# A two-block transformer kernel: 80 of 96 modulation units move from branch A's matmuls to VectorE and ScalarE beside the feed-forwards

## The chip, the cores and the metric

The kernel runs on one core of one Trainium2 chip. The metric is the device time of one execution in microseconds (us). Before the change three runs took 2449.18, 2457.3 and 2463.91 us, median 2457.3.

## The reference, cut to what matters

256 tokens of width 1024 go through a first block of two layers and a second block of two layers, all in fp32. A layer of the first block has three mixing branches (A a recurrent scan, B a chunked linear attention, C a sparse attention), a merge, and a feed-forward with a width-3 convolution over time. The second block modulates each layer by a vector that depends only on a condition `c`:

```
cond = silu(c)                                        # (1024,)
for layer in range(2):
    mod = cond @ ada_w[layer] + ada_b[layer]          # 1024 x 6144 each
    sh1, sc1, g1, sh2, sc2, g2 = split(mod, 6)
    h = rms_norm(x) * (1 + sc1) + sh1
    x = x + g1 * hybrid_mixer(h, ...)                 # GLA heads and retention heads
    x = x + g2 * ffn(rms_norm(x) * (1 + sc2) + sh2)   # layer 0 dense, layer 1 eight experts

def conv_glu(h):                                      # first block
    up = pad(h @ w_up)                                # 2 before the first token
    c = conv_b + sum(conv_w[j] * up[:, j:j + seq] for j in range(3))
    gate, val = split(c)
    return (silu(gate) * val) @ w_down                # hidden width 2816
```

In the mixer, the 16 columns `ga` of the projection feed `log_sigmoid(ga @ w_alpha + b_alpha)`, the decay of the GLA heads.

## The kernel before, in words

Activations lie with the channels on the partitions, 8 tiles of 128 by 256 tokens. Weights come in units of 128x1024 fp32 (512 KB). SyncE loads them in one fixed order (`ORDER.loads`) into `ring`, which has six slots: load n waits until unit n-6 has been used. Most are split units (kind "s"). To keep fp32 accuracy, each is split in two on the way: ScalarE rounds it to `w_high` (`high_to`, L1746), VectorE subtracts to get `w_low` (`low_to`, L2276), each into one of six slots again, and TensorE runs 24 matmuls of 256 columns for it: high by high, high by low, low by high for 8 pieces. ScalarE may round unit n only after TensorE has multiplied unit n-6, VectorE may take it after ScalarE, TensorE after VectorE.

Each engine's program is written out by hand and runs in that order, so what stands behind a wait waits too. The places that matter here:

- Branch A (`branch_a` in the programs of TensorE, VectorE and ScalarE) is a chain of small products of 64x64 whose results are taken out of PSUM by ScalarE or VectorE before the next may begin. Between its steps `mod_point` puts work that doesn't depend on it: the modulation matmuls. A raw unit (kind "r", not split) holds 128x1024 of `ada_w`; TensorE multiplies it with a column of `cond` broadcast to 32 columns (tiles `ring`, `cond` in the trace). 48 units a layer, in three rounds of 16, four at a point; after each round ScalarE copies the bank to `rope`, TensorE transposes it, ScalarE takes it to `mod`.
- The feed-forwards (`feed_forward`) run over 22 groups of 128 hidden channels, three units a group: two up (gate and value) and one down. TensorE runs up(j), then down(j-2). ScalarE, per group: rounds three units, waits for up(j), writes gate and value with bias (L2066, L2067), waits for VectorE's taps, Sigmoid (L2069), waits for the product, rounds it to `hid_high` (L2075). VectorE, per group: three `w_low`, then the taps (four operations of 254 or 255 columns, L2317) once ScalarE has written gate and value, two multiplications (L2308), `hid_low`. The feed-forward of the second block has no taps.
- In the second block's mixer (`linear_attention`) TensorE computes `ga` with 16 plain fp32 matmuls whose weights have 16 columns (`w_ga`, from the tile of constants), VectorE copies it out, and two matmuls give alpha.

Of the kernel before, what the change touches and what calls it, by code (L numbers as in the profile page):

```python
# [33 lines left out]
def _columns(table, sizes):  # L34
# [13 lines left out]
    ("ret_g", 4), ("ret_b", 4), ("w_ga", 128), ("w_alpha", 256)])  # L48
# [64 lines left out]

class Order:
# [5 lines left out]
    RAW1 = MOD_UNITS + 1  # L120
    QK2, RQK2, RV2, GV2, GR2, RG2, OUT2, FEED2 = 0, 4, 12, 16, 20, 24, 28, 36

    def __init__(self):
        self.loads = []
        for layer in range(LAYERS):
            self._load("s", self.layer1(layer), self.A_V)
            self._load("r", layer * self.RAW1, 1)
            self._load("s", self.layer1(layer) + self.A_V, self.C - self.A_V)
            self._load("r", layer * self.RAW1 + 1, MOD_UNITS)
            self._load("s", self.layer1(layer) + self.C, self.LAYER1 - self.C)  # L130
        for layer in range(LAYERS):
            self._load("s", self.layer2(layer), self.FEED2 + (EXPERTS * EXPERT_UNITS if layer else 3 * FF_GROUPS))
# [38 lines left out]
    @staticmethod  # L171
    def fed_ahead(j, groups):

        return 5 if j == 0 else min(3 * j + 4, 3 * groups - 1)

# [72 lines left out]
class Rounds:  # L248

    ROUND = 2 * KT

    def __init__(self):
        self.taken, self.stage = 0, 0

    def more(self, n):
        r, at = self.stage // 3, self.stage % 3
        if at == 1:
            self.stage += 1  # L260
            return r, True, range(0)
        if at:
            return r, False, range(0)
        first, self.taken = self.taken, min(self.taken + n, (r + 1) * self.ROUND, MOD_UNITS)
        return r, False, range(first, self.taken)

    def out(self):
        r, at = self.stage // 3, self.stage % 3
        if (at == 0 and self.taken == (r + 1) * self.ROUND) or at == 2:
            self.stage += 1  # L270
            return r, at
        return r, None

    def open(self):
        return self.stage < 3 * MOD_UNITS // self.ROUND


# [6 lines left out]
        "turned0 turned1 turned2",  # L284
    "mod_act":
        "full0 out0 full1 out1 full2 out2",
# [88 lines left out]
        "ga alpha swapped0 sc00 sc01 sc10 sc11 swapped1 turned s0 s1 s2 intra0 intra1 kturned0 y kturned1 rs0 "  # L375
# [84 lines left out]
def build(nc, a_x, a_pos, a_cond, a_const, a_par1, a_par2, a_router, a_norms, a_weights, a_moe, a_out):  # L460
# [167 lines left out]
    for w in tmps:  # L628
# [49 lines left out]


# [60 lines left out]
    of_mod, of_a, of_b, of_c, of_merge, of_ffn, of_add = (  # L740
        [stage(name, layer) for layer in range(LAYERS)]
        for name in ("mod", "a", "b", "c", "merge", "ffn", "add"))
# [54 lines left out]
    def tensor_program():  # L797
# [99 lines left out]
        def mod_point(M, A, rounds, layer, n=4):  # L897
            r, turn, units = rounds.more(n)
            if turn:
                pe.wait_ge(*M.act(f"full{r}"))  # L900
                for i in range(4):
                    ins = pe.transpose(psum[7][:, i * P:(i + 1) * P], rope[:, i * P:(i + 1) * P], c_("ident"))
                ins.then_inc(*M.pe.mark(f"turned{r}"))
            for j in units:
                k, block = j % Rounds.ROUND // 2, j % 2
                if j % Rounds.ROUND == 0:
                    pe.wait_ge(*(M.act(f"out{r - 1}") if r else A.dve("kk_scaled")))
                raw = layer * ORDER.RAW1 + 1 + j
# [8 lines left out]
        def branch_a(R, A, M, side, layer):  # L917
            s0, rounds, VT = ORDER.layer1(layer), Rounds(), PA[:, 8:12, :]
# [42 lines left out]
            low = layer * ORDER.RAW1  # L961
# [434 lines left out]
        def linear_attention(L, side, layer):  # L1396

            wga = par2(layer, "w_ga").rearrange("p (k r) -> p k r", r=16)
# [81 lines left out]
            fill(side, 3)  # L1480
# [215 lines left out]
        for layer in range(LAYERS):  # L1696
            R, M, A, B, C, G = (d[layer] for d in (of_mix, of_mod, of_a, of_b, of_c, of_merge))
# [19 lines left out]
        for layer in range(LAYERS):  # L1717
            L, s0 = of_lin[layer], ORDER.layer2(layer)
            if layer:
# [3 lines left out]
            begin(of_mix2[layer].dve, [(one.s, half(one.bank, 0), True), (one.s + 1, half(one.bank, 1), False),  # L1723
                                       (two.s, half(two.bank, 0), True)])
# [11 lines left out]
    def scalar_program():  # L1736
# [75 lines left out]
        def branch_a(A, M, side, layer):  # L1812
            s0, a, rounds = ORDER.layer1(layer), A.act, Rounds()
            WA, GD = PA[:, 12, :], PA[:, 13, :]

            def point():
                rounds.more(4)
                r, step = rounds.out()
                if step == 0:
                    act.wait_ge(s_raw, layer * ORDER.RAW1 + (r + 1) * Rounds.ROUND + 1)  # L1820
                    act.activation(rope, psum[7][:, :], Copy).then_inc(*M.act.mark(f"full{r}"))
                elif step == 2:
                    act.wait_ge(*M.pe(f"turned{r}"))
                    src = psum[7][:, :].rearrange("p (i q s) -> p q i s", i=4, q=4)[:, :, :, 0:1]
                    dst = mod[:, 16 * r:16 * r + 16].rearrange("p (q i o) -> p q i o", q=4, o=1)
                    act.activation(dst, src, Copy).then_inc(*M.act.mark(f"out{r}"))
# [32 lines left out]
            act.wait_ge(s_raw, layer * ORDER.RAW1 + 1)  # L1859
# [195 lines left out]
        def feed_forward(F, s0, groups, conv=None, ahead=False, rotary=None):  # L2055
            for j in range(groups):
# [18 lines left out]
                act.activation(HH[:, ts_], HD[n], Copy).then_inc(*f.mark("high"))  # L2075
                if rotary is not None and j == 3:
                    act.wait_ge(*rotary.dve("angle"))
                    act.activation(rope[:, T:2 * T], angle, Sin).then_inc(*rotary.act.mark("sin"))
                    act.activation(reduced, angle, Sin, scale=0.5).then_inc(*rotary.act.mark("half_sin"))
            if ahead:  # L2080
# [136 lines left out]
        for layer in range(LAYERS):  # L2217
            s0 = ORDER.layer1(layer)
            R, M, A, B, C, G = (d[layer] for d in (of_mix, of_mod, of_a, of_b, of_c, of_merge))
# [20 lines left out]
            feed_forward(of_conv[layer], s0 + ORDER.FEED, FF_GROUPS, layer, ahead=True,  # L2240
# [3 lines left out]
        for layer in range(LAYERS):  # L2244
# [10 lines left out]
            if layer == 0:  # L2255
                feed_forward(of_feed, s0 + ORDER.FEED2, FF_GROUPS, ahead=True)
# [10 lines left out]
    def vector_program():  # L2267
# [138 lines left out]
        def branch_a(A, M, side, layer):  # L2406
# [147 lines left out]
            dve.wait_ge(*M.act("out2"))  # L2554
            copy(d, raw_mod[:, layer * MOD_UNITS:(layer + 1) * MOD_UNITS], mod)
# [288 lines left out]
        def feed_forward(F, S, s0, groups, conv=None, scale=None, ahead=False, rotary=None):  # L2844
            for j in range(groups):
# [3 lines left out]
                low_to(s0 + ORDER.fed_ahead(j, groups))  # L2849
                if conv is not None:  # L2850
                    tap = lambda i: par1(conv, "taps", j * TAPS + i)
                    dve.wait_ge(*F[j].act("taken"))
                    for back in (1, 2):
                        for h, (out, src) in enumerate(((CG[n], gate), (CV[n], value))):
                            if back == 2:
                                dve.wait_ge(f.sem, f.last()[1] - 1)
                            stt(f, out[:, back:T], src[:, 0:T - back], tap(4 * h + 2 - back), out[:, back:T], MUL, ADD,
                                "read" if back == 2 and h else "-")
                    dve.wait_ge(*F[j].act("sig"))
# [3 lines left out]
                else:  # L2863
# [3 lines left out]
                    tt(f, HD[n], SG[n], value, MUL, "product")  # L2867
                dve.wait_ge(*F[j].act("high"))
# [13 lines left out]
        def linear_attention(L, side, layer, last):  # L2882
# [35 lines left out]
            dve.wait_ge(*L.pe("ga"))  # L2918
# [255 lines left out]
        def modulation(S, layer):  # L3174
            d = S.dve
            tt(d, mod, raw_mod[:, layer * MOD_UNITS:(layer + 1) * MOD_UNITS], par2(layer, "ada_b"), ADD)
# [9 lines left out]
        for layer in range(LAYERS):  # L3186
            s0 = ORDER.layer1(layer)
            R, M, A, B, C, G = (d[layer] for d in (of_mix, of_mod, of_a, of_b, of_c, of_merge))
# [18 lines left out]
            feed_forward(of_conv[layer], of_add[layer], s0 + ORDER.FEED, FF_GROUPS, layer, ahead=True,  # L3207
# [4 lines left out]
        for layer in range(LAYERS):  # L3212
# [11 lines left out]
            if layer == 0:  # L3224
                feed_forward(of_feed, of_add2, s0 + ORDER.FEED2, FF_GROUPS, scale=lambda dt: mod[:, 40 + dt:41 + dt],
# [160 lines left out]
```

## Time and profile before

| | |
|---|---|
| median of 3 runs | 2457.3 us |
| the profiled execution | 2458.52 us, its span 2457.1 us, about 1.4 us around it |
| TensorE (PE) busy | 2270.8 us, 92% |
| VectorE (DVE) busy | 1602.9 us, 65% |
| ScalarE (ACT) busy | 1174.1 us, 48% |
| HBM read | 423.08 MB, 173 GB/s over the span |
| granted TensorE clock | 0.958 of full on the mean |

TensorE's matmuls are pipelined: one of 256 columns is shown with 0.28 us, but the next starts 0.12 us after it. So durations of matmuls are read from start to start. The feed-forwards of the first block lie at about 472 to 663 us and 1128 to 1320 us, that of the second at 1495 to 1690 us; branch A lies at about 20 to 175 us and 680 to 829 us, and the points with modulation matmuls in it from 64.6 us and from 719.8 us on.

### The profile page before, as it was taken

What the parts mean: (1) busy time and instruction counts of PE and PEld (TensorE: products, weight loads), DVE (VectorE), ACT (ScalarE), POOL (GpSimd) and SP (SyncE); (2) the same over time, 40 slices, a digit from 0 to 9 for tenths busy, and PEclk for the clock granted to TensorE, in tenths of its full rate; (3) what the DMA queues carried; (4) which work ended last, traced back from release to release, by engine and by line L of the source; (5) the groups of instructions that cost most, each with busy time, mean ns of one, the idle gap of its engine ahead of it and who ended that gap; (6) DMA issues with size and microseconds to landing.
All of it is one profiled execution on the core that took longest, in us unless ns stands there. A gap on an engine that the chain in (4) does not pass through costs nothing.

```text
span 2457.1 us, 44886 instructions
## 1 busy us (share of the span) xinstructions
PE 2270.8 (92%) x19011; PEld 2046.4 (83%) x19011; DVE 1602.9 (65%) x2442; ACT 1174.1 (48%) x1703; POOL 0.2 (0%) x4
## 2 busy tenths in 40 slices
PE   7789788999998888889999989999989999999998
PEld 7469788999976787889998989998988888877776
DVE  6537776688773587666776756555765554477886
ACT  5234534455552354344655435444444443456665
POOL 0000000000000000000000000000000000000000
PEclk9999898999999998989998989999988999999999
DMA  5664333355446542334654425563413554579995
GB/s 206 250 237 157 114 103 112 129 198 194 150 172 240 209 145 86 120 111 139 196 199 137 143 64 179 181 185 135 145 35 111 191 182 181 176 271 324 322 327 194
DMA packets 118634, 427.06 MB, mean 174 GB/s; under 512 B 13344, under 2 KB 16160, under 8 KB 118304
## 3 DMA queue, kind: packets, MB, share of 16 engines
q1 hardware_dynamic: 116016, 421.81, 50.0%
q8 instruction: 150, 2.46, 0.4%
q10 hardware_dynamic: 2416, 2.37, 0.3%
q14 instruction: 52, 0.43, 0.1%
HBM read 423.08 MB, written 1.05 MB: 173 GB/s over the span
## 4 chain that ended last, share of the span: by engine, by line
PE 76%; DVE 15%; ACT 5%; issue 3%; DMA 2%; SPq 0%; ACTq 0%; DVEq 0%
PE bank L801 75%; DVE w_low L2276 4%; DVE arena L2308 4%; DMA ring<-in_weights 2%; DVE arena L2317 1%; ACT w_high L1746 1%; DVE y_mix L2308 1%; DVE arena L2813 1%; PE bank L1631 1%; ACT arena L2025 1%; DVE arena L2312 0%; DVE arena L2314 0%; DVE small L2811 0%; DVE arena L2327 0%; ACT arena L1970 0%
## 5 line engine op out<-in xcount | busy, mean ns | idle before, releaser
L2276 DVE TENSOR_TENSOR w_low<-ring,w_high 128x1024 fp32r<-128x1024 f32 x700 | 822.8, 1219 | 156.6 <-ACT w_high L1746 155.8
L1746 ACT ACTIVATE w_high<-ring 128x1024 fp32r<-128x1024 f32 x700 | 699.8, 1051 | 168.8 <-PE bank L801 159.4
L801 PE MATMUL bank<-u_high,w_high 128*128 128x256 f32 x2576 | 740.2, 287 | 29.7 <-DVE u_low L2308 19.7
L801 PE MATMUL bank<-u_low,w_high 128*128 128x256 f32 x2576 | 731.8, 284 | 0.0
L801 PE MATMUL bank<-u_high,w_low 128*128 128x256 f32 x2576 | 731.4, 284 | 0.0
L801 PEld LDWEIGHTS bank<-u_high,w_high 128*128 128x128 f32 x2576 | 496.6, 193 | 43.8 <-issue 35.5
L801 PEld LDWEIGHTS bank<-u_low,w_high 128*128 128x128 f32 x2576 | 496.4, 193 | 0.1
L801 PEld LDWEIGHTS bank<-u_high,w_low 128*128 128x128 f32 x2576 | 495.4, 192 | 0.0
L801 PE MATMUL bank<-arena 64*64 64x64 f32 (+5 forms) x4456 | 240.5, 251 | 77.6 <-issue 20.8
L801 PEld LDWEIGHTS bank<-arena 64*64 64x64 f32 (+2 forms) x4456 | 210.0, 155 | 115.9 <-issue 62.0
L2308 DVE TENSOR_TENSOR arena<-arena 128x256 f32<-128x256 f32 (+3 forms) x218 | 141.7, 666 | 46.7 <-ACT arena L2069 21.3
L801 PE MATMUL bank<-w_high,u_high 128*128 128x256 f32 (+1 forms) x480 | 165.2, 344 | 0.0
L801 PE MATMUL bank<-w_low,u_high 128*128 128x256 f32 (+1 forms) x480 | 162.4, 338 | 0.0
L801 PE MATMUL bank<-w_high,u_low 128*128 128x256 f32 (+1 forms) x480 | 162.1, 338 | 0.0
L801 PE MATMUL bank<-hid_high,w_high 128*128 128x256 f32 x528 | 148.1, 280 | 0.9 <-DVE w_low L2276 0.9
L801 PE MATMUL bank<-hid_high,w_low 128*128 128x256 f32 x528 | 147.9, 280 | 0.0
L801 PE MATMUL bank<-hid_low,w_high 128*128 128x256 f32 x528 | 147.9, 280 | 0.0
L2308 DVE TENSOR_TENSOR turned_low<-bank,turned_high 128x256 fp32r<-128x256 f32 (+1 forms) x66 | 24.8, 399 | 158.5 <-ACT turned_high L2181 158.4
L2181 ACT ACTIVATE turned_high<-bank 128x256 fp32r<-128x256 f32 (+1 forms) x66 | 22.2, 365 | 219.9 <-PE bank L1631 219.9
L1752 ACT ACTIVATE arena<-bank 128x512 f32<-128x512 f32 (+1 forms) x72 | 42.1, 584 | 146.3 <-PE bank L801 146.2
L2317 DVE SCALAR_TENSOR_TENSOR arena<-bank,params,arena 128x255 f32<-128x255 f32 (+1 forms) x204 | 85.4, 474 | 38.5 <-ACT arena L2067 23.3
L801 PE MATMUL bank<-w_high,turned_high 128*128 128x512 f32 x242 | 99.7, 412 | 8.2 <-DVE w_low L2276 7.0
(307 smaller groups left out, 3057.9 us busy)
## 6 DMA issues: line engine op xcount, KB each, us to landing
ring<-in_weights SPq DMA_DIRECT2D x534, 512.0 KB, 4.5
ring<-in_moe SPq DMA_DIRECT2D x264, 512.0 KB, 5.2
const<-in_const SPq DMA_DIRECT2D x1, 2619.0 KB, 16.5
out<-x_res ACTq DMA_DIRECT2D x2, 512.0 KB, 3.0
x_res<-in_x SPq DMA_DIRECT2D x1, 512.0 KB, 5.2
x_res<-in_x ACTq DMA_DIRECT2D x1, 512.0 KB, 5.7
const<-in_par ACTq DMA_DIRECT2D x1, 462.0 KB, 3.4
params<-in_par ACTq DMA_DIRECT2D x1, 247.0 KB, 10.4
```

The costliest lines, as they stand in the source:

```text
L801: return pe.matmul(out, lhsT, rhs, start=start, stop=stop, skip_group_check=loose)
L1631: ins = pe.transpose(bank(q, tile)[:, f * P:(f + 1) * P], hid_e[q % 2][tile][:, f * P:(f + 1) * P], c_("ident"))
L1746: act.activation(WH[:, ORDER.slot[cut], :], weights("s", cut), Copy).then_inc(s_hi, 1)
L1752: act.activation(job.dst, held(job), Copy).then_inc(s_out["act"], 1)
L2025: act.activation(L_c[a][:, h, :], L_c[a][:, h, :], Exp, bias=neg_max[a][:, h:h + 1], accum_out=exp_sum[a][:, h:h + 1]).then_inc(*c.mark(f" ...
L2181: act.activation(HTH[q % 2][tile][:, 0:n], psum[4 + 2 * (q % 2) + tile][:, 0:n], Copy)\
L2276: dve.tensor_tensor(WL[:, b, :], weights("s", cut), WH[:, b, :].bitcast(f32), SUB).then_inc(s_lo, 1)
L2308: dve.tensor_tensor(out, a, b, op).then_inc(*t.mark(name))
L2317: dve.scalar_tensor_tensor(out, a, s, b, op0, op1).then_inc(*t.mark(name))
L2813: dve.match_replace(work_[:, a, 0:n], top8, work_[:, a, 0:n], -3e30).then_inc(*d.mark())
```

## The change

Only round 0 of layer 0 (16 of 96 modulation units) stays in branch A; the other rounds, with their copies to `rope` and transposes, are gone, and so are their loads there. The other 80 come as units of kind "m" in another layout: each holds 128 result channels by 1024, so that VectorE multiplies it with `cond` in a row of 1024 on all partitions (`cond_row`, itself loaded as one more unit per feed-forward) and ScalarE sums over the row (a copy with `accum_out`) into one column of `raw_mod`. They stand in the groups 3 to 21 of the three feed-forwards: 20, 20 and 40 of them. In the first block's feed-forwards `low_to` (three `w_low` a group) moves from before the taps to behind them. The 16 gate columns of GLA become a split unit of their own, padded to 128 columns and begun with the first units of the mixer.

```diff
+    ROUNDS1 = range(0, 1), range(1, 1)
+    ROWS = range(16, 36), range(36, 56), range(56, 2 * MOD_UNITS)
...
+    def _feed(self, g, first):
+        for j in range(FF_GROUPS):
+            before, last = self.fed_ahead(j - 1, FF_GROUPS) if j else -1, self.fed_ahead(j, FF_GROUPS)
+            self._load("s", first + before + 1, last - before)
+            of = self.modulated(g, j)
+            self._load("m", self.row1(g) + of[0] if len(of) else 0, len(of))
+    def modulated(self, g, j):
+        n = len(self.ROWS[g])
+        if j < 3:
+            return range(j == 1)
+        return range(1 + n * (j - 3) // (FF_GROUPS - 3), 1 + n * (j - 2) // (FF_GROUPS - 3))
...  TensorE, linear_attention
-            for k in range(KT):
-                for part in (UH, UL):
-                    ins = mm(psum[0][0:16, 0:T], wga[:, k, :], part[:, k, :].bitcast(f32),
-                             k == 0 and part is UH, k == KT - 1 and part is UL)
-            ins.then_inc(*L.pe.mark("ga"))
-            fill(side, 1)
             pe.wait_ge(*L.dve("ga"))
...
-            fill(side, 3)
+            fill(side, 4)
...  ScalarE, feed_forward
+            def row(j):
+                K, at = of_rows[g], ORDER.row1(g)
+                if j == 1:
+                    act.wait_ge(*arrived("m", at))
+                    act.activation(cond_row, weights("m", at), Sigmoid).then_inc(*K.act.mark("cond"))
+                for i in ORDER.modulated(g, j) if j > 2 else ():
+                    act.wait_ge(*K.dve(f"product{i}"))
+                    col = ORDER.ROWS[g][i - 1]
+                    act.activation(products[i % 3], products[i % 3], Copy, accum_out=raw_mod[:, col:col + 1])\
+                        .then_inc(*K.act.mark(f"sum{i}"))
...
                 act.activation(HH[:, ts_], HD[n], Copy).then_inc(*f.mark("high"))
+                row(1 if j == 1 else j - 1 if j > 3 else 0)
...  VectorE, feed_forward
-                low_to(s0 + ORDER.fed_ahead(j, groups))
+                if conv is None:
+                    low_to(s0 + ORDER.fed_ahead(j, groups))
                 if conv is not None:
...
+                    low_to(s0 + ORDER.fed_ahead(j, groups))
                     dve.wait_ge(*F[j].act("sig"))
...
                     tt(f, HD[n], SG[n], value, MUL, "product")
+                row(j)
                 dve.wait_ge(*F[j].act("high"))
```

ScalarE in the first block's feed-forward, one group from one `hid_high` to the next, before:

```order
L2075 ACTIVATE hid_high<-arena 128x256
L1746 ACTIVATE w_high<-ring 128x1024 x3
L2066 ACTIVATE arena<-bank,params 128x256
L2067 ACTIVATE arena<-bank,params 128x256
L2069 ACTIVATE arena<-arena 128x256
L2075 ACTIVATE hid_high<-arena 128x256
```

and now (L2126 is `hid_high`, L2104 the sum over the row of the group before, L1786 `w_high`, L2117 and L2118 gate and value, L2120 the Sigmoid):

```order
L2126 ACTIVATE hid_high<-arena 128x256
L2104 ACTIVATE arena,raw_mod<-arena 128x1024
L1786 ACTIVATE w_high<-ring 128x1024 x3
L2117 ACTIVATE arena<-bank,params 128x256
L2118 ACTIVATE arena<-bank,params 128x256
L2120 ACTIVATE arena<-arena 128x256
L2126 ACTIVATE hid_high<-arena 128x256
```

Nothing moved there but the sum, which came in ahead of the three roundings. VectorE in the same group, before (the first row is `w_low`, the second and third the taps, the fourth the two multiplications):

```order
L2276 TENSOR_TENSOR w_low<-ring,w_high 128x1024 x3
L2317 SCALAR_TENSOR_TENSOR arena<-bank,params,arena 128x255 x2
L2317 SCALAR_TENSOR_TENSOR arena<-bank,params,arena 128x254 x2
L2308 TENSOR_TENSOR arena<-arena 128x256 x2
L2308 TENSOR_TENSOR hid_low<-arena,hid_high 128x256
```

and now:

```order
L2371 SCALAR_TENSOR_TENSOR arena<-bank,params,arena 128x255 x2
L2371 SCALAR_TENSOR_TENSOR arena<-bank,params,arena 128x254 x2
L2330 TENSOR_TENSOR w_low<-ring,w_high 128x1024 x3
L2362 TENSOR_TENSOR arena<-arena 128x256 x2
L2362 TENSOR_TENSOR arena<-ring,arena 128x1024
L2362 TENSOR_TENSOR hid_low<-arena,hid_high 128x256
```

The three `w_low` now stand between the taps and the multiplications, and the product of the modulation unit between these and `hid_low`. TensorE in branch A of layer 1, where points follow each other most closely (`ring,cond` is a point's eight matmuls, `arena` and `const` the chain's), before:

```order
L801 MATMUL bank<-arena 64x64 x48
L801 MATMUL bank<-ring,cond 32x512 x8
L801 MATMUL bank<-arena 64x64 x16
L801 MATMUL bank<-ring,cond 32x512 x8
L801 MATMUL bank<-const,arena 64x64 x16
```

and now:

```order
L846 MATMUL bank<-arena 64x64 x96
L846 MATMUL bank<-const,arena 64x64 x16
```

The products of the chain now stand directly behind each other: 96 are the 32 ahead of the first of three points, the 48 and the 16.

## Rows read from the trace of the kernel before

**Rows 1.** The chain that ended last, shares of the span by engine.

```profile
PE 76%; DVE 15%; ACT 5%; issue 3%; DMA 2%; SPq 0%; ACTq 0%; DVEq 0%
```

**Rows 2.** Stretches: length, busy PE, PEld, DVE, ACT, POOL; clock, DMA share, GB/s.

```profile
486.00:586.00 100.00, 98.82 (x839) 98.41 (x838) 79.75 (x128) 59.48 (x90) 0.00 (x0) 1.00 0.55 185
586.00:662.00 76.00, 76.00 (x650) 76.00 (x649) 55.18 (x92) 41.02 (x62) 0.00 (x0) 1.00 0.52 174
1500.00:1690.00 190.00, 190.00 (x1604) 190.00 (x1603) 110.40 (x143) 89.90 (x123) 0.00 (x0) 1.00 0.55 172
```

**Rows 3.** ACT in order of time, first feed-forward: start, length, [idle before <-releaser].

```profile
485.33 0.56 ACT L2066 ACTIVATE arena<-bank,params 128x256 f32<-128x256 f32 x1 [6.34 <-PE bank L801]
...
499.34 0.55 ACT L2066 ACTIVATE arena<-bank,params 128x256 f32<-128x256 f32 x1
...
504.04 0.42 ACT L2075 ACTIVATE hid_high<-arena 128x256 fp32r<-128x256 f32 x1 [0.95 <-DVE arena L2308]
504.36 2.94 ACT L1746 ACTIVATE w_high<-ring 128x1024 fp32r<-128x1024 f32 x3
507.20 0.55 ACT L2066 ACTIVATE arena<-bank,params 128x256 f32<-128x256 f32 x1
507.65 0.55 ACT L2067 ACTIVATE arena<-bank,params 128x256 f32<-128x256 f32 x1
...
645.59 0.56 ACT L2066 ACTIVATE arena<-bank,params 128x256 f32<-128x256 f32 x1 [1.07 <-PE bank L801]
...
654.04 0.56 ACT L2066 ACTIVATE arena<-bank,params 128x256 f32<-128x256 f32 x1 [2.98 <-PE bank L801]
```

**Rows 4.** DVE in order of time, one group of the first feed-forward.

```profile
497.57 3.50 DVE L2276 TENSOR_TENSOR w_low<-ring,w_high 128x1024 fp32r<-128x1024 f32 x3 [0.53 <-ACT w_high L1746]
500.99 1.64 DVE L2317 SCALAR_TENSOR_TENSOR arena<-bank,params,arena 128x255 f32<-128x255 f32 x4
503.12 0.89 DVE L2308 TENSOR_TENSOR arena<-arena 128x256 f32<-128x256 f32 x2 [0.48 <-ACT arena L2069]
```

**Rows 5.** Groups by line and shape: busy, mean ns of one, idle before.

```profile
L2308 DVE TENSOR_TENSOR arena<-arena 128x1024 f32<-128x1024 f32 x41 | 49.5, 1220 | 5.7 <-ACT arena L2040 4.7 <-ACT arena L1792 0.4
L1970 ACT ACTIVATE arena<-arena 128x1024 f32<-128x1024 f32 x10 | 10.6, 1056 | 47.0 <-DVE arena L2308 47.0
L2025 ACT ACTIVATION_READ_ACCUMULATOR arena<-arena,small 128x1 f32 x32 | 6.0, 187 | 0.0
L801 PE MATMUL bank<-ring,cond 128*32 128x512 f32 x384 | 64.3, 638 | 14.4 <-DMA ring<-in_weights 7.2 <-DVE arena L2308 5.2 <-ACT mod L1826 1.5
```

**Rows 6.** PE in order of time, branch A of layer 1.

```profile
728.45 1.05 PE L801 MATMUL bank<-ring,cond 128*32 128x512 f32 x4 [0.61 <-DMA ring<-in_weights]
...
732.65 2.51 PE L801 MATMUL bank<-arena 64*64 64x64 f32 x78 [0.53 <-DVE arena L2308]
...
760.71 1.92 PE L801 MATMUL bank<-ring,cond 128*32 128x512 f32 x16
762.56 3.02 PE L801 MATMUL bank<-arena 64*64 64x64 f32 x96
...
769.44 1.05 PE L801 MATMUL bank<-ring,cond 128*32 128x512 f32 x4
...
774.61 1.15 PE L801 MATMUL bank<-const,arena 64*64 64x64 f32 x32
...
811.60 1.54 PE L801 MATMUL bank<-arena 64*64 64x64 f32 x43 [4.54 <-issue]
```

**Rows 7.** What PE waited for: us in total, times, longest us.

```profile
PE bank L801 <- issue: 21.2, 12, 4.5
```

**Rows 8.** Stretches, as in rows 2: clock in branch A, and the gate columns.

```profile
810.00:820.00 10.00, 8.40 (x170) 5.06 (x170) 1.96 (x6) 0.78 (x2) 0.00 (x0) 0.66 0.44 152
...
1345.40:1352.10 6.70, 6.70 (x32) 2.92 (x30) 1.07 (x2) 0.90 (x1) 0.00 (x0) 1.00 0.64 237
```

**Rows 9.** GB/s in the 40 slices of the span.

```profile
GB/s 206 250 237 157 114 103 112 129 198 194 150 172 240 209 145 86 120 111 139 196 199 137 143 64 179 181 185 135 145 35 111 191 182 181 176 271 324 322 327 194
```

More of the change, by code:

```diff
@@ L111, in constants, with __init__, more, out @@
     return c
+class Rounds:
+    ROUND = 2 * KT
+    def __init__(self, rounds):
+        self.first, self.last = rounds.start, rounds.stop
+        self.taken, self.stage = self.ROUND * self.first, 3 * self.first
+    def more(self, n):
+        r, at = self.stage // 3, self.stage % 3
+        if at == 1:
+            self.stage += 1
+            return r, True, range(0)
+        if at:
+            return r, False, range(0)
+        first, self.taken = self.taken, min(self.taken + n, (r + 1) * self.ROUND, self.last * self.ROUND)
+        return r, False, range(first, self.taken)
+    def out(self):
+        r, at = self.stage // 3, self.stage % 3
+        if (at == 0 and self.taken == (r + 1) * self.ROUND) or at == 2:
+            self.stage += 1
+            return r, at
+        return r, None
+    def open(self):
+        return self.stage < 3 * self.last
 class Order:
@@ L245, in made @@
         return jobs
[L248 to L275, printed above, removed]
 STEPS = {
@@ L677, in build @@
     CG, CV, SG, HD = ([new(T) for _ in TWO] for _ in range(4))
+    cond_row, products = at(32 * T, 4 * T), [at((36 + 4 * n) * T, 4 * T) for n in range(3)]
     space(0)
@@ L2079, in feed_forward @@
                     act.activation(reduced, angle, Sin, scale=0.5).then_inc(*rotary.act.mark("half_sin"))
+            row(groups - 1)
             if ahead:
@@ L2842, in branch_c, with feed_forward, row @@
             branches_b_c(B, C, G, level, probabilities, side, layer, last)
-        def feed_forward(F, S, s0, groups, conv=None, scale=None, ahead=False, rotary=None):
+        def feed_forward(F, S, s0, groups, g, conv=None, scale=None, ahead=False, rotary=None):
+            def row(j):
+                K, at = of_rows[g], ORDER.row1(g)
+                if j == 2:
+                    dve.wait_ge(*K.act("cond"))
+                    tt(K.dve, cond_row, cond_row, weights("m", at), MUL, "cond")
+                    prior(K.dve)
+                for i in ORDER.modulated(g, j) if j > 2 else ():
+                    dve.wait_ge(*arrived("m", at + i))
+                    if i > 3:
+                        dve.wait_ge(*K.act(f"sum{i - 3}"))
+                    tt(K.dve, products[i % 3], weights("m", at + i), cond_row, MUL, f"product{i}")
             for j in range(groups):
@@ L3175, in modulation @@
             d = S.dve
+            for n in (0, 1) if layer == 0 else (2,):
+                dve.wait_ge(*of_rows[n].act.end())
+            if layer == 0:
+                dve.wait_ge(*of_mod.act("out"))
             tt(d, mod, raw_mod[:, layer * MOD_UNITS:(layer + 1) * MOD_UNITS], par2(layer, "ada_b"), ADD)
```

114 lines of the change are left out of this document (67 added, 47 removed), and 13 rows, old and new, of the table STEPS.

## The prediction

> **What bounds the kernel now.** Read the chain of waits first. 76% of the span is TensorE and 15% VectorE [rows 1], so the time is TensorE's stream of work plus the places where it stands. Then the stretches. In the first block's feed-forward TensorE is busy all the time at full clock, VectorE 80% in the first part and 73% later, ScalarE 59 and 54% [rows 2]. By these shares there is room for more work beside the matmuls. The order of events inside one group shows how little. Up to some 580 us the gate writes of two groups start 7.86 us apart (499.34 and 507.20) and nothing there waits for TensorE; at the end they are 8.45 us apart (645.59 and 654.04) and each waits over 1 us for TensorE [rows 3]. So TensorE needs 8.45 us for three units (2.81 each), and ScalarE and VectorE, handing work to each other, need 7.86 us for a group. They wait for each other most of the rest of their time; the room is 0.6 us a group, not the 25% that the busy share leaves.
>
> **The loop in the first block's feed-forwards.** Before, VectorE's three w_low (3.42 us from start to start of what follows, 497.57 to 500.99) run while ScalarE still rounds the second and third unit and writes gate and value [rows 3, 4]. Afterwards they cannot: the taps stand ahead of them, the taps wait for gate and value, these stand behind three roundings, and the roundings behind hid_high of the group before. Walk round one full group, from the start of the gate write:
> - gate and value written: 1.05 (507.20 to the end of the second, 507.65 + 0.55) [rows 3]
> - taps, until the next may start: 1.57 (1.64 less the 0.07 by which neighbours overlap) [rows 4]
> - three w_low, now in the chain: 3.42 [rows 4]; the Sigmoid lies beside them, so its 0.48 is gone
> - two multiplications and the hand-over: 0.92 [rows 4]
> - hid_high: 0.33 (504.04 to 504.36) [rows 3]
> - the sum over the modulation row: a ScalarE operation of 128x1024 takes 1.056, its successor starts 0.1 earlier, and reading the accumulator (0.187 by itself) costs about 0.1 so overlapped [rows 5]: 1.05. The bound from below is 0.95, from above 1.25.
> - three roundings: 2.84 (504.36 to 507.20) [rows 3]
>
> The sum is 11.2 us where TensorE needs 8.45. The product of the modulation unit on VectorE (1.22 [rows 5]) lies where VectorE would wait for ScalarE (5.3 us from product to taps, against 1.2 + 0.4 of work), so it costs nothing. Without modulation rows the loop would be 10.1: moving w_low alone already makes it longer than TensorE's 8.45.
>
> A feed-forward has 22 groups. From the first gate write to the last, 21 steps, it takes 168.7 us now (485.33 to 654.04) [rows 3], and three units of TensorE behind that. Afterwards: the first two steps are short of one w_low each and of the sum (8.0 and 10.0); step 3 is 13.7, because the load six places behind the cond unit waits for VectorE to use that unit in group 2, and lands late for group 3's last rounding; step 4 is 10.1; then 16 of 11.2; the last 9.3. That is 230, and about 10 from the last gate write to TensorE's end instead of 8.4: +63. In the second layer 2 us of it were lost already to work on the rotary tables in the same loop, so +63 and +62, **+125**. Behind each, ScalarE's last sum and three roundings come before the squares of the norm: about 1 us each, **+2**. A row's cost of 0.95 or 1.25 would move the pair by -4 or +8.
>
> **The second block's feed-forward** has no taps; w_low stays at the front. The loop there: hid_high 0.33, two sums 2.1, one rounding 0.97, three w_low 3.42, multiplications 0.92, hand-over: 7.8, under 8.45 [rows 3 to 5]. TensorE stays the bound, nothing is added. 5.1 loads of 0.524 MB per 8.45 us are 317 GB/s, and the trace shows 322 to 327 held over slices [rows 9], so it fits barely: **+1**, bounds 0 and +9 (if only 300 GB/s come).
>
> **Branch A.** The modulation matmuls hold TensorE 64.3 us, and it stood 14.4 us before them [rows 5]: 78.7 for 96 units, 65.6 for the 80 that go. Not all comes back, since they also covered hand-overs. Taken point by point in layer 1: the first two points (719.8 to 732.65) return only 3.2, because VectorE's own chain to the masked products, started at the operation after "at", lets the next product begin at 729.4 instead of 732.65 [rows 6]. Where the chain's results are ready, a point returns all: 1.85 (760.71 to 762.56), 5.2 for the one that waited for loads (769.44 to 774.61) [rows 6]. All points of layer 1: 31.4, less 1.7 for two hand-overs that come bare (AKV0's copy 0.8, the last Pm's addition 0.85): 29.7. Layer 0, rounds 1 and 2: 25.2 less 2.0. Together 53. Against that two things: TensorE stands for instructions ("issue") 12 times, 21.2 us, all but little of it in stretches of small products [rows 7]; without the long matmuls more such waits come into the open, at a mean of 1.8 us I take three. And such a gap goes ahead of a fall of the clock: after 4.54 us without instructions the granted clock of 810 to 820 us is 0.66 [rows 6, 8], some 3 us lost in ten; once more. I take **-47**, between -35 and -55.
>
> **Gate columns.** 32 passes with 16-column weights take 6.7 us [rows 8]; the padded unit takes 2.81. But alpha now follows directly, while VectorE first takes out a bank (0.6) and then ga (0.4): TensorE stands 1.1 us where a side job of 5.6 us covered it. -2.8 a layer, **-5.6**.
>
> **Sum.** 125 + 2 + 1 - 47 - 5.6 = +75. On the profiled execution's 2458.5 us (span 2457.1), which lies 1.2 above the median, that is 2534; against the median 2533. I forecast 2534.
>
> **Rivals.**
> - TensorE stays the bound of the convolution's feed-forwards, faster. VectorE's work per group is 6.3 us and becomes 7.5, ScalarE's 4.7 becomes 5.7, both under 8.45 [rows 2, 4]. It needs ScalarE to be able to write gate and value before VectorE's product of the group before, which the written order forbids. Time: 2458.5 - 47 - 5.6 = 2406. By the Trainium skill, "Perfetto Trace Analysis", section "Identifying the Most-Contended Engine", the busy share of VectorE and ScalarE is a fair measure of how close they are to their limit; by that rule this rival would hold. The 7.86 us loop at 80% busy [rows 2, 3] speaks against reading it so here. 6%.
> - Slower loop, smaller: the sum over the row hides (ScalarE waits for something else at that point), the step is 10.1: 2 x 19 x 1.05 less, 2494. Nothing in rows 3 shows such a wait. 8%.
> - The clock falls in the feed-forwards. TensorE now stands 2.7 us in every group, and in branch A a gap of 4.5 went ahead of a fall [rows 6, 8]. As long as half clock lasts a third of the time, the 2.7 us that TensorE has to spare take it. If it is half throughout, three units take 16.9 us, and 2 x 20 x 5.7 are added: 2760; if half of the groups are hit so, 2648. 6%. The Trainium skill, "TensorE: Matmul & The Clock Gate", section "HAM oscillation — how this bites in real kernels", tells of a kernel in which waits between bursts cooled the clock every time; it speaks for this rival, and the rows only show single falls.
> - Branch A gives little: waits for instructions and for VectorE fill the room. -20 instead of -47: 2561. Rows 7 speak for it, the rows of layer 1 where results lay ready against. 10%.
> - Loads bind in both kinds of feed-forward (landing late behind the modulation units): +9 in the second block, about +15 in each of the others if a load takes 7 us: 2573. 8%.
>
> **Numbers.** My case has 62% and a range of its own of 2515 to 2552. The range 2494 to 2570 takes in the second rival and the fourth; out of it are the first, the third, the far half of the last. 0.5% is 12 us, about what a measurement of this kernel can tell. Slower by more than that 0.92, within it 0.02, faster 0.06.
>
> **What would show it.** In the first block's feed-forwards gate writes 11.2 us apart, with TensorE waiting 2.7 us per group for w_low, and VectorE waiting some 3.5 us for gate and value ahead of the taps. In the second block's 8.45 and no such wait. Branch A of layer 1 some 30 us shorter from kk_spread to y, of layer 0 some 23, less the waits for instructions. I am wrong if the steps are 8.45, if ScalarE's sum takes much over 1.1, or if branch A keeps its length.

## The result, and the profile after

The changed kernel takes 2511.3 us (median of 4 runs, 2507.77 to 2514.61) against 2456.33 before, a ratio of 1.0225 with a 95% interval of 1.0207 to 1.0243. I had forecast 2534: slower was right and the time inside the range of 2494 to 2570, but the change costs 55 us where I had summed 75, and 2511 lies 4 us under the range of 2515 to 2552 that I gave my own case. One execution of all that follow, of a1, took 4267.44 us and is left out of its ratio. The profiled execution has a span of 2507.2 us, 50.1 more than before. First the stages, each from one mark on ScalarE to the next (the root of a norm, the copy of branch A's y), in us:

| stage | before | after | difference | forecast |
|---|---|---|---|---|
| branch A, layer 0 | 163.3 | 136.2 | -27.1 | |
| branch A, layer 1 | 161.4 | 118.3 | -43.2 | both: -47 |
| first feed-forward | 197.6 | 263.6 | +66.0 | |
| second feed-forward | 203.4 | 264.3 | +61.0 | both: +127 |
| third feed-forward | 196.3 | 200.7 | +4.4 | +1 |
| second block's two mixers | 331.9 | 321.4 | -10.5 | -5.6 |
| all the rest | | | -0.5 | 0 |

The chain that ended last, shares of the span by engine, now:

```profile
PE 63%; DVE 21%; ACT 12%; issue 3%; DMA 1%; ACTq 0%; DVEq 0%; SPq 0%
```

TensorE's share fell from 76% [rows 1] to 63, ScalarE's rose from 5 to 12 and VectorE's from 15 to 21: in part of the program the time now belongs to these two. Which part shows in ScalarE's order of time in the first feed-forward (start, length, idle before and what ended it):

```profile
532.01 0.54 ACT L2117 ACTIVATE arena<-bank,params 128x256 f32<-128x256 f32 x1
532.46 0.55 ACT L2118 ACTIVATE arena<-bank,params 128x256 f32<-128x256 f32 x1
534.72 0.42 ACT L2120 ACTIVATE arena<-arena 128x256 f32<-128x256 f32 x1 [1.72 <-DVE arena L2371]
538.92 0.42 ACT L2126 ACTIVATE hid_high<-arena 128x256 fp32r<-128x256 f32 x1 [3.78 <-DVE arena L2362]
539.24 1.04 ACT L2104 ACTIVATE arena<-arena 128x1024 f32<-128x1024 f32 x1
540.20 0.18 ACT L2104 ACTIVATION_READ_ACCUMULATOR arena<-arena 128x1 f32 x1
540.28 2.94 ACT L1786 ACTIVATE w_high<-ring 128x1024 fp32r<-128x1024 f32 x3
543.13 0.55 ACT L2117 ACTIVATE arena<-bank,params 128x256 f32<-128x256 f32 x1
```

and VectorE in the same group:

```profile
533.04 1.65 DVE L2371 SCALAR_TENSOR_TENSOR arena<-bank,params,arena 128x255 f32<-128x255 f32 x4 [3.80 <-ACT arena L2118]
534.61 3.48 DVE L2330 TENSOR_TENSOR w_low<-ring,w_high 128x1024 fp32r<-128x1024 f32 x3
538.01 0.88 DVE L2362 TENSOR_TENSOR arena<-arena 128x256 f32<-128x256 f32 x2
538.80 1.22 DVE L2362 TENSOR_TENSOR arena<-ring,arena 128x1024 f32<-128x1024 f32 x1
539.94 0.42 DVE L2362 TENSOR_TENSOR hid_low<-arena,hid_high 128x256 fp32r<-128x256 f32 x1
544.16 1.65 DVE L2371 SCALAR_TENSOR_TENSOR arena<-bank,params,arena 128x255 f32<-128x255 f32 x4 [3.80 <-ACT arena L2118]
```

Each engine waits for the other and neither for TensorE. The gate writes lie 11.12 us apart (532.01 and 543.13) where they lay 7.86 and 8.45 apart [rows 3]; the sum in the forecast was 11.2. ScalarE stands 3.78 us before hid_high, where it stood 0.95 [rows 3]: in that time VectorE does the three w_low that used to lie beside the roundings (534.61 to 538.01) and the two multiplications. The sum costs 1.04 with its accumulator (539.24 to 540.28). TensorE's waits show the same from its side (us in total, times, longest), before and then after:

```profile
PE bank L801 <- DVE w_low L2276: 13.7, 13, 1.5
```

```profile
PE bank L846 <- DVE w_low L2330: 88.5, 49, 3.9
...
PE bank L846 <- issue: 8.6, 7, 2.4
```

The last row is the surprise ("issue": TensorE waits for nothing but its next instructions): these waits were 21.2 us in 12 [rows 7]; I had expected more of them, and there are fewer.

### The profile page after: what moved, and what is told of

Read it like the earlier page. It is cut to its first block, busy times and chain, and to the rows that moved or that the text cites. A ratio compares the mean times of both kernels' runs of the same rounds, so it can differ in the third digit from the quotient of the medians.

```text
span 2507.2 us, 44491 instructions
## 1 busy us (share of the span) xinstructions
PE 2247.1 (90%) x18655; PEld 2066.1 (82%) x18655; DVE 1686.7 (67%) x2525; ACT 1253.9 (50%) x1858; POOL 0.2 (0%) x4
## 3 DMA queue, kind: packets, MB, share of 16 engines
HBM read 425.57 MB, written 1.05 MB: 170 GB/s over the span
## 4 chain that ended last, share of the span: by engine, by line
PE 63%; DVE 21%; ACT 12%; issue 3%; DMA 1%; ACTq 0%; DVEq 0%; SPq 0%
PE bank L846 61%; DVE w_low L2330 7%; ACT w_high L1786 5%; DVE arena L2362 5%; DVE arena L2371 4%; ACT arena L2104 2%; DVE y_mix L2362 1%; ACT arena L2118 1%; ACT arena L2117 1%; DMA ring<-in_weights 1%; DVE arena L2865 1%; PE bank L1669 1%; ACT arena L2065 1%; DVE arena L2368 0%; DVE small L2863 0%
## 5 line engine op out<-in xcount | busy, mean ns | idle before, releaser
L846 PE MATMUL bank<-u_high,w_high 128*128 128x256 f32 x2592 | 759.9, 293 | 103.8 <-DVE w_low L2330 78.3
L1786 ACT ACTIVATE w_high<-ring 128x1024 fp32r<-128x1024 f32 x702 | 701.0, 1051 | 155.5 <-PE bank L846 136.2
L846 PE MATMUL bank<-u_low,w_high 128*128 128x256 f32 x2592 | 748.0, 289 | 0.0
L846 PE MATMUL bank<-u_high,w_low 128*128 128x256 f32 x2592 | 747.6, 288 | 0.0
L846 PEld LDWEIGHTS bank<-u_high,w_high 128*128 128x128 f32 x2592 | 511.1, 197 | 123.3 <-DVE w_low L2330 86.6
L846 PEld LDWEIGHTS bank<-u_low,w_high 128*128 128x128 f32 x2592 | 511.6, 197 | 0.1
L846 PEld LDWEIGHTS bank<-u_high,w_low 128*128 128x128 f32 x2592 | 510.8, 197 | 0.0
L846 PE MATMUL bank<-arena 64*64 64x64 f32 (+5 forms) x4456 | 233.4, 247 | 70.9 <-DVE arena L2374 19.4
L846 PEld LDWEIGHTS bank<-arena 64*64 64x64 f32 (+2 forms) x4456 | 204.8, 151 | 96.4 <-issue 39.9
L2234 ACT ACTIVATE turned_high<-bank 128x256 fp32r<-128x256 f32 (+1 forms) x66 | 22.2, 365 | 218.1 <-PE bank L1669 218.1
L2126 ACT ACTIVATE hid_high<-arena 128x256 fp32r<-128x256 f32 x66 | 27.6, 418 | 185.6 <-DVE arena L2362 185.6
L846 PEld LDWEIGHTS bank<-hid_high,w_high 128*128 128x128 f32 x528 | 101.8, 193 | 8.6 <-issue 7.1
```

The lines of the kernel that those rows point to most:

```text
L846: return pe.matmul(out, lhsT, rhs, start=start, stop=stop, skip_group_check=loose)
L1786: act.activation(WH[:, ORDER.slot[cut], :], weights("s", cut), Copy).then_inc(s_hi, 1)
```

## The experiments

The first four take the loop of the first block's feed-forwards apart, the next two branch A, then come the gate columns and two versions that are meant to be fast.

**a1: w_low ahead of the taps again.**

```diff
-                if conv is None:
-                    low_to(s0 + ORDER.fed_ahead(j, groups))
+                low_to(s0 + ORDER.fed_ahead(j, groups))
...
-                    low_to(s0 + ORDER.fed_ahead(j, groups))
                     dve.wait_ge(*F[j].act("sig"))
```

> The changed kernel with the three w_low put ahead of the taps again; the modulation rows stay. Theory (the loop of hand-overs between ScalarE and VectorE sets the step): one group is hid_high 0.33, the sum 1.05, the first rounding 1.05, three w_low 3.42, taps 1.57, Sigmoid and hand-over 0.56, two multiplications 0.92, about 8.9 us where the changed kernel has 11.12. The 21 steps of a first-block feed-forward take about 186 us instead of 228 and 230, so some 85 us less in all: 2422, ahead of the kernel before. Rival (the modulation units themselves, their loads and products, hold the loop): steps stay at 10 us or more and the time at 2470 or more.

Measured: 2420.24 us, ratio to before 0.9849 (0.9829 to 0.9868). The steps are 8.90 us, and the 21 of them take 181.9 and 185.3. So the same 80 units beside the same feed-forwards make the kernel 1.5% faster than before once w_low stands where it stood. The rival, that the units themselves hold the loop at 10 us or more, is out.

**a2: as a1, and the sum in ScalarE's wait for the taps.**

```diff
                     act.activation(CV[n], value, Ident, bias=tap(7), scale=tap(6)).then_inc(*f.mark("taken"))
+                    if j > 3:
+                        row(j - 1)
...
-                row(1 if j == 1 else j - 1 if j > 3 else 0)
+                row(1 if j == 1 else j - 1 if j > 3 and conv is None else 0)
```

> As a1, and ScalarE does the sum over the modulation row behind gate and value, where it waits 1.7 us for the taps, instead of ahead of the roundings. Theory: the sum leaves the loop, which falls to 7.9 us, under TensorE's 8.45; steps as before the change (7.87, later 8.45), gate writes of a feed-forward some 170 us from first to last, 2390 in all. Rival 1 (loads bind, 4.05 a group): steps of 8.6 to 9, 2400 to 2415. Rival 2 (VectorE's product of 1.2 comes into the loop instead, since it now has less to wait for): steps about 9, 2425.

Measured: 2401.09 us, 0.9771 (0.9755 to 0.9787). ScalarE in order of time:

```profile
539.03 0.54 ACT L2117 ACTIVATE arena<-bank,params 128x256 f32<-128x256 f32 x1
539.48 0.55 ACT L2118 ACTIVATE arena<-bank,params 128x256 f32<-128x256 f32 x1
539.93 1.05 ACT L2104 ACTIVATE arena<-arena 128x1024 f32<-128x1024 f32 x1
540.88 0.19 ACT L2104 ACTIVATION_READ_ACCUMULATOR arena<-arena 128x1 f32 x1
542.36 0.42 ACT L2122 ACTIVATE arena<-arena 128x256 f32<-128x256 f32 x1 [1.28 <-DVE arena L2373]
543.73 0.42 ACT L2128 ACTIVATE hid_high<-arena 128x256 fp32r<-128x256 f32 x1 [0.95 <-DVE arena L2364]
544.05 2.94 ACT L1786 ACTIVATE w_high<-ring 128x1024 fp32r<-128x1024 f32 x3
546.89 0.55 ACT L2117 ACTIVATE arena<-bank,params 128x256 f32<-128x256 f32 x1
```

The sum lies in a wait, 1.28 of which is left, and the step is 7.86 (539.03 to 546.89), the one of before to the hundredth. From the middle of the feed-forward on TensorE sets the step, now 8.54 where it was 8.45. That 0.1 I can't explain, but it isn't the added work: the third feed-forward has 8.54 in the kernel before and 8.45 in the changed one, and c2 has 8.54 with nothing added to its feed-forwards. The 21 steps take 172.9 and 175.3 us, against 168.7 and 171.9 before; of the 11 us over what I expected, 8 are these, for which I had taken 170 each, and 3 are not placed. The time is the one that the rival of binding loads gave (2400 to 2415), but its steps of 8.6 and more from the start are not there: most of the first half goes at 7.86.

**a3: taps first as in the change, only the sum in the gap.**

```diff
+                    if j > 3:
+                        row(j - 1)
                     act.wait_ge(*F[j].dve("read"))
```

> The changed kernel, taps first as in it, with only the sum moved behind gate and value on ScalarE. Theory: the loop keeps w_low and loses the sum: 10.07 us a step, 18 steps by 1.05 us less in each of two feed-forwards: 2507 - 38 = 2469. Rival (the sum lies beside something else and the step has another cause): steps stay at 11.1, 2505.

Measured: 2478.05 us, 1.0088 (1.0072 to 1.0105). Steps of 10.09: the sum's price in the loop is 11.12 - 10.09 = 1.03. The time fell by 33 us, not 38. The steps give 17.7 and 17.4, since 17 of them are shorter by 1.03 where I had counted 18 by 1.05; the other 2 us are not placed.

**b1: the kernel before, only w_low behind the taps.**

```diff
+                if conv is None:
+                    low_to(s0 + ORDER.fed_ahead(j, groups))
-                low_to(s0 + ORDER.fed_ahead(j, groups))
...
+                    low_to(s0 + ORDER.fed_ahead(j, groups))
                     dve.wait_ge(*F[j].act("sig"))
```

> The kernel before with only the three w_low moved behind the taps in the first block's feed-forwards; the modulation stays in branch A. Theory: steps of 10.07 us instead of 7.87 and 8.45, the 21 steps about 207 instead of 169 and 172: +36 each, 2530. Rival (the order of VectorE costs nothing as long as it is under 80% busy): 2457, steps at 8.45.

Measured: 2529.65 us, 1.0291 (1.0274 to 1.0308). Steps of 10.08 without a single modulation unit in the feed-forward. One edit of two lines costs more than the whole change does; the rest of the change gives some 16 us back (1.0291 against 1.0225).

**c1: the kernel before without the loads of the modulation units.** The matmuls stay and read a resident tile, so the modulation values are not the reference's.

```diff
-            self._load("r", layer * self.RAW1 + 1, MOD_UNITS)
...
-                pe.wait_ge(*arrived("r", raw))
...
-                             weights("r", raw)[:, h * 512:(h + 1) * 512], k == 0, k == KT - 1)
+                             ones, k == 0, k == KT - 1)
```

> The kernel before with the 96 loads of modulation units left out; TensorE's modulation matmuls stay, in number and shape, and read a resident tile of constants, so the modulation values aren't the reference's. Theory (TensorE's waits for instructions in branch A are fetches held up by the weight loads): the 21.2 us in 12 waits of this kind fall below 8, those of layer 1's branch A from 11.0 to about 2, and the 7.2 us of waits for loads go too: some 20 us less, 2437. Rival (they come with the number of small matmuls in a row, whatever the loads do): the waits for instructions stay at 18 or more, and 2450.

Measured: 2411.22 us, 0.9821 (0.9802 to 0.984), twice as much as expected. Every modulation matmul is there, a point's 16 records take 1.92 us in a row, as the undisturbed ones did before, and yet branch A is 24.5 us shorter in layer 0 and 24.0 in layer 1.

**c2: the other half, all loads and hardly a matmul.** Behind the first unit pair of a round only 16 of 512 columns are multiplied; the modulation values are not the reference's.

```diff
+                n = 16 if k else 512
...
-                    ins = mm(psum[7][32 * q:32 * q + 32, :], cond[:, k:k + 1].to_broadcast([P, 32]),
-                             weights("r", raw)[:, h * 512:(h + 1) * 512], k == 0, k == KT - 1)
+                    ins = mm(psum[7][32 * q:32 * q + 32, 0:n], cond[:, k:k + 1].to_broadcast([P, 32]),
+                             weights("r", raw)[:, h * 512:h * 512 + n], k == 0, k == KT - 1)
```

> The kernel before with all loads, but of the modulation matmuls behind the first of a round only 16 of 512 columns are multiplied, so the modulation values aren't the reference's. Theory (fetches held up by loads): TensorE's waits for instructions stay at 15 us or more although nearly all long matmuls are gone, and waits for loads grow, since 48 units want over 58 us a layer; branch A returns clearly less than in the changed kernel (27 and 43 us): about 35 in all, 2422. Rival (without the long matmuls the waits shrink whatever is loaded): under 8 us of such waits, and 2400 or less.

Measured: 2447.02 us, 0.9961 (0.9945 to 0.9976); with nearly all of the matmuls gone only 8.1 us came back in layer 0 and 3.7 in layer 1. I had expected 35 in all. TensorE's waits for instructions, in c1 and then in c2:

```profile
PE bank L800 <- issue: 1.0, 1, 1.0
```

```profile
PE bank L801 <- DMA ring<-in_weights: 24.4, 21, 2.3
...
PE bank L801 <- issue: 19.2, 11, 4.2
```

With loads and few long matmuls there are 11, with matmuls and no loads there is 1: nearly all of them come with the loads. Layer 1's branch A as stretches (length, busy PE, PEld, DVE, ACT, POOL; clock, DMA share, GB/s), of the kernel before, c1, c2 and the changed kernel:

```profile
719.00:829.00 110.00, 92.18 (x2132) 62.37 (x2132) 41.39 (x80) 26.19 (x47) 0.00 (x0) 0.95 0.67 252
```

```profile
692.00:780.00 88.00, 80.37 (x2140) 58.84 (x2132) 43.07 (x84) 28.23 (x50) 0.00 (x0) 1.00 0.09 33
```

```profile
714.00:820.00 106.00, 78.99 (x2132) 68.54 (x2132) 41.51 (x80) 26.01 (x47) 0.00 (x0) 0.82 0.69 261
```

```profile
757.00:825.00 68.00, 57.79 (x1928) 53.39 (x1928) 41.26 (x80) 24.52 (x42) 0.00 (x0) 0.97 0.10 37
```

The two with 250 GB/s and more are the long ones, 106 and 110 us; the one with all matmuls and 33 GB/s takes 88. In c2 the clock is down to 0.82, TensorE standing for loads 24.4 us in all, so a part of its length is clock and not the waits themselves.

**c3: only the gate columns as a padded unit.**

```diff
-            for k in range(KT):
-                for part in (UH, UL):
-                    ins = mm(psum[0][0:16, 0:T], wga[:, k, :], part[:, k, :].bitcast(f32),
-                             k == 0 and part is UH, k == KT - 1 and part is UL)
-            ins.then_inc(*L.pe.mark("ga"))
-            fill(side, 1)
             pe.wait_ge(*L.dve("ga"))
```

> The kernel before with only the gate columns as a padded unit. Theory: 32 passes of 6.7 us become one unit of 2.8, and 1.1 us of waiting for the copy comes into the open: -2.8 a layer, 2452. Rival (one more unit to round and subtract at the mixer's start delays the first projection, and eats it): 2457.

Measured: 2450.49 us, 0.9986 (0.9972 to 1.0): some 4 us, and at the edge of what can be told from nothing. In its profile the two mixers of the second block are 3.1 and 3.4 us shorter, where -2.8 each was forecast; but stages that the edit doesn't touch differ from the kernel before by up to 2.3 us there too.

**d1: as a2, with no modulation left in branch A.**

```diff
-    ROUNDS1 = range(0, 1), range(1, 1)
-    ROWS = range(16, 36), range(36, 56), range(56, 2 * MOD_UNITS)
+    ROUNDS1 = range(0, 0), range(0, 0)
+    ROWS = range(0, 24), range(24, 48), range(48, 2 * MOD_UNITS)
```

> As a2 (w_low first, sum in the gap), and the last 16 modulation units leave branch A of layer 0 too: 24, 24 and 48 rows beside the three feed-forwards. Theory: branch A of layer 0 gets 12 to 15 us shorter; the five groups with two rows in each first-block feed-forward take 9.0 instead of 8.5, +5 in all; the second block's feed-forward wants 5.5 loads in 8.45 us, 341 GB/s where 327 were held, +7: about 2398, the same as a2 or a little less. Rival (the waits for instructions there stay where they are, and loads cost over 10): 2405 or more.

Measured: 2387.72 us, 0.9717 (0.9697 to 0.9738). That is 10 us under the 2398 expected. Branch A of layer 0 is 16.3 us shorter than in a2, where 12 to 15 was expected, and TensorE's waits for instructions are 2.9 us in 2 where a2 had 9.3 in 8. The three of a2 that stand beside loads in layer 0 (1.70, 2.43 and 1.09 us) are gone; the two that are left, 1.61 and 1.24, have no weight load beside them.

**e1: as d1, the last group's sums and products out of the tail.**

```diff
-            row(groups - 1)
             if ahead:
                 high_to(s0 + 3 * groups + 2)
+            return lambda: row(groups - 1)
...  ScalarE, squares of the norm: the sums behind them
+            late()
...  VectorE, feed_forward
-                row(j)
+                if j < groups - 1:
+                    row(j)
...
                 tt(f, HL[:, ts_], HD[n], HH[:, ts_].bitcast(f32), SUB, "hidden")
+                if j == groups - 1:
+                    row(j)
```

> As d1, and at the end of each feed-forward ScalarE does the last group's sums behind the squares of the norm, where it waits for TensorE anyway, and VectorE the last group's products behind hid_low. Theory (the sums and products of the last group lie in the chain from the last gate write to the norm, which is 6.9, 6.9 and 5.6 us longer in the changed kernel than before): 2 to 3 sums of 1.04 and 2 to 3 products of 1.14 leave that chain three times: 3 to 4 us each, some 10 in all, 2378. Rival (TensorE's last products and the clock set the tail, the sums lie beside them): 2388, as d1.

Measured: 2375.61 us, 0.9665 (0.9648 to 0.9682), 3.4% faster than the kernel before. Of the changed kernel, ScalarE behind the last group:

```profile
685.84 0.54 ACT L2117 ACTIVATE arena<-bank,params 128x256 f32<-128x256 f32 x1
...
690.81 1.04 ACT L2104 ACTIVATE arena<-arena 128x1024 f32<-128x1024 f32 x1
...
691.85 1.04 ACT L2104 ACTIVATE arena<-arena 128x1024 f32<-128x1024 f32 x1
...
692.88 1.04 ACT L2104 ACTIVATE arena<-arena 128x1024 f32<-128x1024 f32 x1
...
693.93 2.94 ACT L1786 ACTIVATE w_high<-ring 128x1024 fp32r<-128x1024 f32 x3
...
705.76 0.26 ACT L1827 ACTIVATE rstd<-bank,steady 128x2 f32<-128x2 f32 x1 [4.93 <-PE bank L846]
```

and of e1:

```profile
613.02 0.56 ACT L2118 ACTIVATE arena<-bank,params 128x256 f32<-128x256 f32 x1 [1.57 <-PE bank L846]
...
617.46 2.94 ACT L1786 ACTIVATE w_high<-ring 128x1024 fp32r<-128x1024 f32 x3
...
621.82 2.54 ACT L1822 ACTIVATE arena<-x_res 128x256 f32<-128x256 f32 x8
624.27 1.04 ACT L2105 ACTIVATE arena<-arena 128x1024 f32<-128x1024 f32 x1
...
625.31 1.04 ACT L2105 ACTIVATE arena<-arena 128x1024 f32<-128x1024 f32 x1
...
626.85 0.26 ACT L1828 ACTIVATE rstd<-bank,steady 128x2 f32<-128x2 f32 x1 [0.41 <-PE bank L846]
```

From the last gate write to the root: 19.92 us in the changed kernel, 13.83 here, and 13.01 before (654.04 [rows 3] to 667.05). Against d1 these tails are 5.2 and 3.8 us shorter behind the first two feed-forwards, and the third is shorter by only 1.3 in all, where 3 to 4 each was expected; another 4 us come from the steps of the first two.

## Why the prediction was right, and where not

**The loop: right in its mechanism and its size.** Term by term the walk round one group holds: steps of 11.12 for 11.2 forecast, first steps of 8.03 and 9.89 for 8.0 and 10.0, a last one of 9.23 for 9.3. The third was 12.42 instead of 13.7: ScalarE did wait for a load there, but only 2.22 us. The 21 steps took 227.6 and 229.6 us, +58.9 and +57.7 (forecast 230, +61). b1 and a1 show by themselves what I had only argued: the move costs the time, 72 us alone, and undone in the changed kernel it gives 91. a3 sets the sum at 1.03 (1.05 forecast). That the first two feed-forwards cost 127 us to the microsecond is luck: their steps cost 6 us less than forecast, and their tails (below) about as much more.

**The rival "TensorE stays the bound" fell, and with it the reading by shares.** Before, VectorE was 80% and ScalarE 59% busy [rows 2], in the changed kernel, between 540 and 560 us, 62 and 51%. They are less busy than before and yet the time is theirs:

```profile
540.00:560.00 20.00, 16.74 (x128) 16.34 (x127) 12.37 (x20) 10.16 (x17) 0.00 (x0) 0.91 0.50 177
```

The Trainium skill, "Perfetto Trace Analysis", section "Identifying the Most-Contended Engine", would have the engine of the highest occupancy optimized first, and judges TensorE by its MFU and the busy share of its weight loads. Here that is TensorE, whose weight loads are busy 16.34 of 20 us, though it stands waiting for w_low in these groups. a2 does nearly the same work in the same engines at 7.86 a step, and there VectorE is 92% and ScalarE 67% busy over the same stretch. The measurement decides against the rule here: two engines that hand work back and forth set the time by the length of their loop, at 62 and 51% busy.

**The rival of the falling clock happened and cost nothing in the loop.** The same row has the clock at 0.91; at 683 us the matmuls follow each other at 0.21 instead of 0.12. The step stayed 11.12 throughout, for TensorE had 2.7 us a group to spare, as the prediction put it (one such wait is shown with 2.4). It cost in the first tail, where nothing is spare:

```profile
698.74 6.99 PE L846 MATMUL bank<-steady,arena 128*128 128x1 f32 x32 [2.45 <-ACT arena L1822]
```

Before, the same 32 took 3.73; the granted clock of 698 to 706 us is 0.54.

**The tails: mis-sized.** I took one sum behind the last group, +1 a feed-forward, and about 1.6 for the rest. There are three sums in the first two and five in the third, and two products ahead of the last hid_low: +6.9 from the last gate write to the root in the first, +3.9 in the second, +5.6 in the third, where I had 0 to 1 (and 6.9 for the second too, in what I expected of e1). Of the 6.9, 3.1 are the three sums and 3.3 the slow clock just told. e1 takes the sums and products out of that chain and gains 12 us in all (forecast 10).

**Branch A: the step that failed.** "without the long matmuls more such waits come into the open, at a mean of 1.8 us I take three", and "some 3 us lost in ten; once more": I took off 6 us (53 to 47), and the sign was wrong: branch A got 70.3 us shorter, where I had 47 and at most 55. These 23 us are nearly the whole of the 25 by which the sum missed the profile. I had seen the waits for instructions stand among small products and made these their cause. They stand there, but what makes most of them, and makes them long, is the loads. In the twelve us around the longest one of before, at 811.6 [rows 6], the DMA queues are (packets, MB, share of 16 engines):

```profile
q1 hardware_dynamic: 1056, 3.81, 83.7%
q8 instruction: 2, 0.03, 1.0%
```

The instructions come over the same DMA engines, two packets beside 1056 of weights. That the waits are for them is shown: each of the 41 in the kernel before, the changed one, a2, c1, c2 and d1 ends 1.2 to 1.6 us after a packet of q8 has landed. That most of them leave with the loads and not with the matmuls is shown too, by c1 (1 wait), c2 (11), d1 (2) and by the changed kernel, where layer 0's first round kept its loads and its waits (1.73, 2.44 and 1.27 us, before 2.00, 2.45 and 0.98) and layer 1 fell from 11.0 to 1.7 us. That the instruction packets queue behind the weights is only argued; once started, the one that ends a wait takes 0.88 to 1.11 us before and 0.93 in c1. And a part of what I had forecast is there: the changed kernel has four such waits where no weights move at all. Two of them, and all that the queues carry in the 11 us around them:

```profile
136.41 0.80 PE L846 MATMUL bank<-arena 64*64 64x64 f32 x38 [0.60 <-issue]
...
140.02 0.70 PE L846 MATMUL bank<-arena 64*64 64x64 f32 x29 [0.90 <-issue]
```

```profile
q8 instruction: 2, 0.03, 1.1%
```

The other two are 1.01 and 0.66 us. So small products alone do run out of instructions, at 0.8 us a time where I had taken 1.8; the waits of 2 to 4.5 us stand beside loads.

So layer 1's branch A comes apart in two steps: 161.4 before, 137.4 without loads, 118.3 without loads and matmuls. In this order the loads were worth 24.0 and the matmuls, with their copies and transposes, 19.1. The split hangs on the order: with the loads still there, c2 got only 3.7 for nearly all of the matmuls. My pointwise sum for layer 1 was 29.7, part matmuls and part waits for loads. Of the 24.0, 10 us are waits for instructions. Another 11 are the twelve points themselves, from the first modulation matmul to the chain's next product: 33.5 us before, 22.2 in c1, 1.85 each. The waits for loads that are listed in them are only 2.6 us of it: behind each the matmuls start anew, four are shown with 1.05 where 16 in a row take 1.92, and so the point of 769.44 took 5.17 [rows 6] with 1.03 of listed waits. Some 1.7 is the half clock at 813.07 (3.64 for 1.92). The 3 us of the 24.0 that are left I can't place.

**Gate columns: right in size, as far as one profile tells.** -2.8 a layer forecast, -3.1 and -3.4 in c3's profile, and 4 us for both in its median. The mixers of the changed kernel are 5.9 and 4.6 us shorter; the rest of it stays open.

**The rival of binding loads** showed nothing: in the third feed-forward TensorE sets the step, 8.45; the last gate write comes 1.2 us earlier than before, and the tail is 5.6 longer.

## What to carry to other kernels

Before work is put beside a bound engine, walk once round the loop of hand-overs of the engines that feed it; the room is the difference between that loop and the bound engine's time, not the idle share. Added work goes where its engine waits for its partner inside the loop: the same sum cost 1.03 us a group ahead of the roundings and nothing behind the gate writes. And work whose weights stream can cost the stretch that it stands in more than its matmuls: take the loads away alone before pricing the matmuls. Four edits that each follow from a row (w_low first, the sum in the gap, the rest of the loads out of branch A, the last sums behind the squares) took the same change from 2.2% slower to 3.4% faster.

## What the runs showed of the hardware that I had not expected

TensorE's waits for instructions follow the weight traffic: 12 waits of 21.2 us in the kernel before, 1 of 1.0 with the same matmuls and 33 instead of 252 GB/s in branch A, 11 of 19.2 with the loads and hardly a long matmul. Each ends 1.2 to 1.6 us after an instruction packet of 16 KB has landed. Where no weights move they are 0.4 to 1.6 us long, beside weights up to 4.5.
